# The fourth layer's modulation made in the second layer's merge

## The reference, cut to what matters

```python
# first block, layers 1 and 2
shift_x, scale_x, gate_x = jnp.split(jax.nn.silu(c) @ w_mod + b_mod, 3, axis=-1)
hx = rms_norm(xs, norm_g) * (1 + scale_x[:, None]) + shift_x[:, None]
...
xs = xs + gate_x[:, None] * merge(px, ya_x, yb_x, yc_x)
# second block, layers 3 and 4: the same with c_2, w_ada, b_ada
...
x = x + gate[:, None, :] * y
```

## Time and profile before

| what | us |
|---|---|
| median of 3 runs (lowest, highest) | 3547.54 (3545.79, 3547.58) |
| the profiled execution | 3549.07 |
| its span, first to last instruction | 3547.0 |
| PE busy, of the span | 3262.0 |
| DVE busy | 1299.8 |
| ACT busy | 822.2 |
| POOL busy | 1431.1 |

### The profile page before, as it was taken

The page is one execution under the profiler, slowest core; times in us unless marked ns, Lnnn a source line. Parts: engine busy times, 40 slices in busy tenths (PEclk is TensorE's granted clock), DMA queues, the critical chain, the costliest instruction groups (busy, mean ns, idle before and its releaser), DMA issues.

```text
span 3547.0 us, 38760 instructions
## 1 busy us (share of the span) xinstructions
PE 3262.0 (92%) x14557; PEld 2232.0 (63%) x14557; DVE 1299.8 (37%) x2414; ACT 822.2 (23%) x1447; POOL 1431.1 (40%) x1372
## 2 busy tenths in 40 slices
PE   5999897879999989987999989999999899999997
PEld 4666564646656546454644438888886378889953
DVE  6210313623444231134532243555552234443322
ACT  2311323611111032223521112232121023322110
POOL 0008988920000000899200017766551167775600
PEclk6999997989999999998999989999999999999998
DMA  6111110003322111210033412222331322222211
GB/s 195 48 36 36 30 36 13 2 24 95 95 89 80 60 60 48 54 36 24 13 105 120 142 49 76 84 84 93 99 107 36 85 72 72 65 67 72 72 52 43
DMA packets 259180, 236.50 MB, mean 67 GB/s; under 512 B 20870, under 2 KB 257202, under 8 KB 258996
## 3 DMA queue, kind: packets, MB, share of 16 engines
q1 hardware_dynamic: 258996, 234.02, 21.8%
HBM read 231.90 MB, written 2.10 MB: 66 GB/s over the span
## 4 chain that ended last, share of the span: by engine, by line
PE 73%; POOL 15%; DVE 7%; issue 2%; ACT 2%; DMA 0%; DVEq 0%; ACTq 0%; SPq 0%; POOLq 0%
PE ps L420 34%; PE ps L953 21%; POOL arena L1977 8%; PE ps L450 8%; POOL posi L1976 4%; PE ps L1003 2%; DVE arena L1482 2%; PE ps L436 1%; PE ps L1047 1%; ACT arena L1095 1%; DVE arena L1486 1%; PE ps L1039 1%; DVE bQz L1486 1%; PE ps L516 1%; DVE small L1650 1%
## 5 line engine op out<-in xcount | busy, mean ns | idle before, releaser
L420 PE MATMUL ps<-hT,wring 128*128 128x512 f32 (+1 forms) x1568 | 577.0, 528 | 1.4 <-ACT arena L1095 1.4
L420 PE MATMUL ps<-arena,wring 128*128 128x512 f32 (+1 forms) x1280 | 491.1, 544 | 10.6 <-DVE arena L1482 10.6
L420 PEld LDWEIGHTS ps<-hT,wring 128*128 128x128 f32 x1568 | 303.2, 195 | 258.6 <-issue 242.4
L2013 POOL TENSOR_TENSOR arena<-wring 128x512 f32<-128x512 f32 x72 | 94.8, 1317 | 839.1 <-DMA wring<-in_w_in 550.4
L1977 POOL TENSOR_TENSOR arena<-arena,posi 128x512 f32<-128x512 f32 (+1 forms) x360 | 405.5, 1126 | 30.1
L450 PE MATMUL ps<-hT,wring 128*128 128x512 f32 (+1 forms) x1088 | 404.6, 526 | 0.0
L420 PEld LDWEIGHTS ps<-arena,wring 128*128 128x128 f32 x1280 | 243.2, 191 | 247.3 <-issue 227.9
L1095 ACT ACTIVATE arena<-ps 128x256 f32<-128x256 f32 (+4 forms) x407 | 183.0, 450 | 748.0 <-PE ps L420 335.9
L450 PEld LDWEIGHTS ps<-hT,wring 128*128 128x128 f32 x1088 | 205.8, 194 | 162.7 <-issue 153.4
L1095 ACT ACT_TABLE_LOAD x146 | 187.3, 1283 | 495.9 <-PE ps L528 95.3
L1482 DVE TENSOR_TENSOR arena<-arena 128x768 f32<-128x768 f32 (+7 forms) x121 | 160.8, 1329 | 364.5 <-ACT arena L1095 361.2
(11 more groups left out here) (187 smaller groups left out, 4291.6 us busy)
## 6 DMA issues: line engine op xcount, KB each, us to landing
wring<-in_w_in SPq DMA_DIRECT2D x128, 1024.0 KB, 5.4
wring<-in_w_mod SPq DMA_DIRECT2D x24, 1024.0 KB, 7.8
wring<-in_w_out SPq DMA_DIRECT2D x24, 1024.0 KB, 5.7
wring<-in_w_ada SPq DMA_DIRECT2D x24, 1024.0 KB, 5.1
wring<-in_w_conv_out SPq DMA_DIRECT2D x8, 512.0 KB, 3.6
wring<-in_w_gla_out SPq DMA_DIRECT2D x8, 512.0 KB, 4.0
wring<-in_w_attn_out SPq DMA_DIRECT2D x8, 512.0 KB, 4.4
arena<-in_x SPq DMA_DIRECT2D x1, 2048.0 KB, 9.7
```

The source lines that it names most:

```text
L420: last = eng.matmul(o_(out), a, b_, start=(i == 0), stop=(i == len(parts) - 1))
L2013: pool.link(eng.tensor_tensor(t1, w[:, 0:4, P:2 * P], w[:, 0:4, 0:P], ALU.subtract))
```

## The change

The 24 groups of layers 3 and 4 are made in the second layer's merge, six per quarter. `mod_places` says at which of a quarter's six places (three gates, three outputs) which group is finished and which is entered for loading; for the first layer it gives the same places as before. For layers 3 and 4 the sums have six buffers of 256 columns, which are all of `bQz`, with a count of their own. `modT` has room for three layers (L % 3). The cell stage has no modulation steps any more.

```diff
@@ def mod_groups(l, a):
-    todo = ([(0, g) for g in range(8, 12)] if l == 0 else []) + [(l + 1, g) for g in range(12)]
+    todo = ([(0, g) for g in range(8, 12)] + [(1, g) for g in range(12)] if l == 0 else
+            [(L, g) for L in (2, 3) for g in range(12)])
     n = len(todo) // 4
     return todo[a * n:(a + 1) * n]
+
+
+def mod_places(l):
+
+    return ([[0], [1], [2], [3], [], []], [[], [0], [1], [2], [3], []]) if l == 0 else (
+        [[0], [1, 2], [3, 4], [5], [], []], [[], [0], [1, 2], [3, 4], [], [5]])
@@ steps2
             yield [("load", n, i), ("products", n, i)]
-            mods = []
-            if i == 0 and 2 <= n < 8:
-                mods = [("mod", n, 2 * n - 3)]
-            elif i == 2 and 1 <= n < 7:
-                mods = [("mod load", n, 2 * n - 2)]
-            elif i == 3 and 1 <= n < 7:
-                mods = [("mod", n, 2 * n - 2), ("mod load", n, 2 * n - 1)]
-            yield [("corners", n, i)] + mods
+            yield [("corners", n, i)]
@@ buffers
-        modT = sb("modT", [P, 2, 24, 2])
+        modT = sb("modT", [P, 3, 24, 2])
...
+        md_one = bQz.rearrange("p a b -> p (a b)").rearrange("p (a b) -> p a b", b=256)
+
+        def mod_sums(L, g, n):
+            return md_one[:, n % 6, :] if L > 1 else (md_first if (L, g) < (0, 8) else md)[:, n % 2, :]
@@ PE, merge, at the gates (at the outputs alike with 3 + b_)
-                        if b_:
-                            mod_finish(*mods[b_ - 1])
-                        mod_load(*mods[b_])
+                        for i in mod_places(l)[1][b_]:
+                            mod_finish(*mods[i])
+                        for i in mod_places(l)[0][b_]:
+                            mod_load(*mods[i])
@@ DVE, modulate
-                i = len(mods_done) % 2
+                done, depth = mods_done[L > 1], 6 if L > 1 else 2
+                all_sums = mod_sums(L, g, len(done))
...
-                if len(mods_done) > 1:
-                    eng.wait_ge(*at(("full", (("mod", mods_done[-2][0]), mods_done[-2][1], 1))))
+                if len(done) >= depth:
+                    eng.wait_ge(*at(("full", (("mod", done[-depth][0]), done[-depth][1], 1))))
@@ PE, ACT and DVE, cell stage
-                    if kind == "mod load":
-                        if l < DEPTH - 1:
-                            mod_load(L + 1, x[0])
-                    elif kind == "mod":
-                        if l < DEPTH - 1:
-                            mod_finish(L + 1, x[0])
...
```

More of the change, by code:

```diff
@@ L510, in mod_finish @@
                 eng.wait_ge(*at(("mod summed", L, g)))
-                i = mod_no[0] % 2
-                mod_no[0] += 1
+                sums = mod_sums(L, g, mod_no[L > 1])
+                mod_no[L > 1] += 1
                 for j in range(2):
@@ L515, in mms @@
                         for c in range(ncol):
-                            last = eng.matmul(o_[:, c:c + 1], (md2 if L > 2 else md_first if (L, g) < (0, 8) else md)[:, i, c * 256 + j * P:c * 256 + (j + 1) * P], ones[:, 0:1],
+                            last = eng.matmul(o_[:, c:c + 1], sums[:, c * 256 + j * P:c * 256 + (j + 1) * P], ones[:, 0:1],
                                               start=True, stop=True)
@@ L519, in mod_finish @@
                     job("A", (("mod", L), g, j), mms)
-            mod_no = [0]
+            mod_no = [0, 0]
             def square_sum(L):
@@ L897, in _ @@
                         used(("full", ("mout", l, a, b_, 1, segs(l)[-1])))
[L898 to L901, removed]
+                        for i in mod_places(l)[1][3 + b_]:
+                            mod_finish(*mods[i])
+                        for i in mod_places(l)[0][3 + b_]:
+                            mod_load(*mods[i])
                 eng.wait_ge(*at(("merged", l, KD - 1)))
@@ L987, in _ @@
                     q, v = qk2[b], vv[b]
-                    if kind == "mod load":
-                        if l < DEPTH - 1:
-                            mod_load(L + 1, x[0])
-                    elif kind == "mod":
-                        if l < DEPTH - 1:
-                            mod_finish(L + 1, x[0])
-                    elif kind == "out":
+                    if kind == "out":
                         j = x[0]
@@ L1118, in modulate @@
                         f = 2 * g + j
-                        evac((("mod", L), g, j), modT[:, L % 2, f, 0:ncol], 0, ncol, ACT.Identity,
+                        evac((("mod", L), g, j), modT[:, L % 3, f, 0:ncol], 0, ncol, ACT.Identity,
                              bias=col(s, B_MOD + f))
@@ L1134, in head_of_layer @@
                         fn(hT[:, k, t0:t0 + n], hT[:, k, t0:t0 + n], ACT.Identity,
-                           ("h ready", L, sg, k), bias=modT[:, L % 2, k, c_:c_ + 1])
+                           ("h ready", L, sg, k), bias=modT[:, L % 3, k, c_:c_ + 1])
             def tiles(name, l, dst, ntile, seg, func=ACT.Identity, b0=None, off=None, first=0):
@@ L1359, in _ @@
                                      bias=col(l, B_M + 8 * b_ + 2 * a + j))
-                        if b_:
-                            modulate(mods[b_ - 1][0], [mods[b_ - 1][1]])
-                            act.stage("merge")
+                        for i in mod_places(l)[1][b_]:
+                            modulate(mods[i][0], [mods[i][1]])
+                        act.stage("merge")
                     for b_ in range(3):
@@ L1367, in _ @@
                                 evac(("mout", l, a, b_, j, sg), my[:, 2 * b_ + j, t0:t0 + n], 0, n)
-                        if b_ < len(mods) - 2:
-                            modulate(mods[2 + b_][0], [mods[2 + b_][1]])
-                            act.stage("merge")
+                        for i in mod_places(l)[1][3 + b_]:
+                            modulate(mods[i][0], [mods[i][1]])
+                        act.stage("merge")
             act.stage("rotary")
@@ L1403, in _ @@
                     h, r, b = n % 4, n // 4, n % 2
[L1404 to L1408, removed]
+                    if kind == "gates":
                         evac(("gcols", l), qcol[:, :, :, :], 0, 64)
@@ L1501, in squares @@
                         tt(rstd[:, t0:t0 + n], rstd[:, t0:t0 + n], hT[:, k, t0:t0 + n], A_, ("squares", L, sg) if k == KD - 1 else None)
-            mods_done = []
+            mods_done = [], []
             def modulate(L, g):
-                i = len(mods_done) % 2
+                done, depth = mods_done[L > 1], 6 if L > 1 else 2
+                all_sums = mod_sums(L, g, len(done))
                 slot, count = mod_slot[L, g]
@@ L1510, in modulate @@
                 eng.wait_ge(m.sem(f"w_slot{slot}"), count)
-                if len(mods_done) > 1:
-                    eng.wait_ge(*at(("full", (("mod", mods_done[-2][0]), mods_done[-2][1], 1))))
+                if len(done) >= depth:
+                    eng.wait_ge(*at(("full", (("mod", done[-depth][0]), done[-depth][1], 1))))
                 ncol, col0 = (2, 0) if L < 2 else (1, 16)
                 for c in range(ncol):
-                    sums = (md2 if L > 2 else md_first if (L, g) < (0, 8) else md)[:, i, c * 256:(c + 1) * 256]
+                    sums = all_sums[:, c * 256:(c + 1) * 256]
                     ts(sums, w[:, 0, :], cT[:, col0 + 8 * c:col0 + 8 * c + 1], None, M_, None)
@@ L1519, in modulate @@
                             ("mod summed", L, g) if (c, k) == (ncol - 1, KD - 1) else None)
-                mods_done.append((L, g))
+                done.append((L, g))
             def norm(L):
@@ L1528, in norm @@
                     nc_ = 2 if L < 2 else 1
-                    stt(gsT[:, :, 0:nc_], modT[:, L % 2, 8:16, 0:nc_], 1.0,
+                    stt(gsT[:, :, 0:nc_], modT[:, L % 3, 8:16, 0:nc_], 1.0,
                         cols[:, s, 0:8].unsqueeze(2).broadcast_to([P, 8, nc_]), A_, M_)
@@ L1771, in _ @@
                         c_ = 0 if sg == "x" else 1
-                        stt(xT[:, j, t0:t0 + n], bank_of[k][:, 0:n], modT[:, l % 2, 16 + j, c_:c_ + 1],
+                        stt(xT[:, j, t0:t0 + n], bank_of[k][:, 0:n], modT[:, l % 3, 16 + j, c_:c_ + 1],
                             xT[:, j, t0:t0 + n], M_, A_, ("free", k))
@@ L1871, in _ @@
                     h, r, b = n % 4, n // 4, n % 2
[L1872 to L1877, removed]
+                    if kind == "products":
                         i = x[0]
@@ L1962, in _ @@
                     eng.wait_ge(*at(("full", k)))
-                    stt(xT[:, j, TC:T], bank_of[k][:, 0:TX], modT[:, L % 2, 16 + j, 0:1], xT[:, j, TC:T], M_, A_, ("free", k))
+                    stt(xT[:, j, TC:T], bank_of[k][:, 0:TX], modT[:, L % 3, 16 + j, 0:1], xT[:, j, TC:T], M_, A_, ("free", k))
                     squares(L + 1, j)
```

1 line of the change is left out of this document (removed).

## The result

The changed kernel takes 3526.34 us (median of 4, 3523.47 to 3527.21) against 3546.86 us for the kernel before on the same occasions (3545.79 to 3547.58): ratio 0.9941, 95% interval 0.9924 to 0.9958. That is 20.5 us faster; 24.0 were forecast, and the time lies in the range. The profiled executions differ by 3549.07 - 3526.76 = 22.3 us, the spans by 3547.0 - 3524.8 = 22.2.

The account below looks back on a forecast made before the run. The prediction took TensorE (PE), busy in 92% of the span, as the bound. Cell stage -28.1 us and merge finishes +4.1 gave -24.0: profiled 3549.07 becomes 3525.1, the median 1.5 lower, 3523.5 us; range 3517 to 3538.

Parts of the forecast that it names:

- The cell's part: Third layer's cell stage: taking out 12 modulation groups saves 28.1 us, bounds 25 to 30.
- The twin layer: Fourth layer's cell stage, same loop and shapes without modulation: head 1 to head 7 takes 452.80 us against 481.60.
- Rival B: Third layer's cell stage keeps half its loss, since PE's order of steps made the twin faster: 3537.6 us, chance 9%.
- Its mechanism: Cell stage: POOL waits 66.8 us for modulation matmuls, 46.2 for w_in loads queued behind groups that DVE sums slowly.
- The finishes in the merge: Second layer's merge: 12 more groups' one-column matmuls on full PE cost 12 x 0.34 = 4.1 us, bounds 3.5 to 5.
- The loads: Second layer's merge: all weight and modulation loads stay hidden, with 1.1 us of slack; 171 GB/s in a quarter.
- the narrowest place: Merge quarter, second output weight's load: issued at 41.7, landed at 48.9, needed at 50.0, 1.1 us to spare.
- M5, W4 and W5: Merge quarter's sixth modulation load, second and third output weight loads; the third might make the second 0.2 us late per quarter.
- DVE in the merge: Second layer's merge: 4.1 us a group with POOL silent, six groups plus merging 30.7 of 64.2 us a quarter.
- Rival C: DVE becomes the merge's bound if sums cost there what they cost in the cell: 3563 us, chance 3%.
- Six buffers: Second layer's merge: with six sum buffers, DVE's 15.3 us wait at a quarter's third group is gone.
- The sum: Whole kernel: -28.1 + 4.1 = -24.0 us, forecast 3523.5 us, chance 70%.

Follow-up runs that it names:

- the finishes alone: Kernel before, its cell-stage fourth-layer groups without loads and six of eight DVE instructions; two on a constant, finish and ACT copies stay: 3526.40 us, ratio 0.9947.
- the spread kernel: Changed kernel with one finish per place, and also one modulation load behind each of a quarter's six weights, against one finish per place only: 3524.72 us, ratio 0.9934.

## Why the prediction was right, point by point

- **The cell's part** (28.1 us forecast): the trace has 30.9, the kernel without the fourth layer's modulation 30.4 by medians. The twin layer was the right measure: 453.2 us where it had 452.8. What the forecast had wrong lies behind the stretch. It took 0.7 us as given back there, and 2.5 more were won: 86.1 us where the kernel before had 88.6 and its twin 89.3. The granted clock there is 1.00 against 0.95 before. Which work sets the clock's lows at that place was not tested. Rival B, half of the gain, is out.
- **Its mechanism** was told half right. I had a w_in load wait in the queue until DVE had summed the group before it. The trace of the kernel before already speaks against that: the loads that POOL waits for went out about 1 us before DVE began, behind another w_in load's slot. The 66.8 us of waits for L516 were counted for the mechanism too, and with the finishes alone POOL waits 84.7. The runs show three causes: the finishes (8 us in the stretch, 10.4 to the landmark behind it), the loads' places in the ring (alone 14 and 11.0 more) and the sums (alone 14 and 11.1 more). That DVE's slow sums stand on the path was right. By which steps they delay PE in detail was not followed. The estimate didn't rest on the mechanism, and so it was not hurt.
- **The finishes in the merge** (12 x 0.34 = 4.1 us): this is the step that failed, in two terms. The size of a finish was taken from its piece in the chain, 0.34 us; a single one costs 0.45, since the first product behind it starts a little later (a quarter grows from 63.14 to 64.48 us for three more). One of the 12 lies in the wait at the end, so 11 x 0.45 = 4.9 us. And the sum took two finishes in a row as twice one, with a lower bound by which two together might even cost less. They wait for ring A's fourth bank: 65.52 - 64.48 = 1.04 us a quarter, 0.52 for each of the eight double finishes, 4.2 us in all, as the kernels with single finishes and with eight banks show. That ACT's two copies of a group "lie beside PE" was true of the copies, and overlooked that the bank which the next finish needs is emptied by the same engine. So 4.9 + 4.2 = 9.1 us and not 4.1, and outside the bounds of 3.5 to 5.
- **The loads** were hidden, as forecast, and the spread kernel gains nothing. At the narrowest place M5, W4 and W5 were issued at 1890.7, 1891.1 and 1891.7 and landed after 5.2, 6.2 and 7.1 us, so W4 was there 6.7 us after M5's issue and not 7.2. That left 2.8 us of slack where 1.1 was worked out. The first was not held up by the later two. The Trainium skill (DMA: Bandwidth & Descriptors, "Queues, rings and completion order") says that each DMA engine consumes the descriptors of a queue in ring order. By that W4 lands in time, as the prediction worked out, and the trace agrees. The pair of the earlier trace rows was read too strongly against it: its first load was of w_in, and a w_in load with no other beside it took 5.7 us in the same merge (issued at 1902.0), so by that measure the later load accounts for 0.7 us of its 6.4 and not for 1.3. The worked schedule had DVE wait for loads, and it does (88.4 us in 13 waits). The DMA rate is 168 GB/s where 171 were worked out.
- **DVE in the merge**: 4.0 us a group (4.1 was a slip in adding the same terms), sums of 483 to 487 ns with POOL silent. Rival C is out.
- **Six buffers** took away the wait of 15.3 us, and that wait was worth nothing.
- **The sum**: 9.1 - 30.9 = -21.8, with -0.4 elsewhere, is the 22.2 us between the spans. That the forecast of 24.0 came close owes something to two errors of opposite sign, 5 us too little for the merge and 2.8 too little for the cell.

## What to carry to other kernels

Where a kernel has two stages on the same shapes and only one carries the work that is to be moved, the difference of the two was here a better price than a sum of instruction times. When small matmul jobs are put side by side on a full PE, count the PSUM banks that the row of jobs asks for, and who empties them, before counting matmul time; eight banks or one job at a time took the wait away. And the few microseconds where PE must wait anyway, at the end of a stage, are the cheapest place for such jobs.

## What the runs showed that I had not expected

Loads and sums taken away one at a time show 7 us each in the stretch, and both at once 20.6; to the next landmark it is 9.5 and 9.4 against 20.5. An overlap read from one stretch can lie in the granted clock in part, so the landmark behind it should be read as well, with the clock beside it.

The time behind the third layer's stretch, for the same instructions, goes with the granted clock: 86.1 to 86.2 us in the seven traces of all 13 where it was 1.00, 88.6 to 88.9 in the five where it was 0.95 or 0.96. Behind the fourth layer's stretch the two don't go together as closely: 89.3 to 89.5 us both at 0.94 and at 0.96. So a part of what a change seems to win at a landmark may be the clock's, and perhaps the 2.5 us won behind the stretch here.
